# A MoE down projection turned round: tokens stationary, w_down streamed in two fp32r halves

## The reference

```
logits = xf @ w_router + b_router;  top 4 of 32 experts, softmax over the four logits
gu     = x_e @ w_gate_up[e] + b_gate_up[e]                 # 1024 -> 2048, gate and up interleaved
gate   = min(gu[:, 0::2], 7);  up = clip(gu[:, 1::2], -7, 7)
hidden = (up + 1) * gate * sigmoid(1.702 * gate)
y      = hidden @ w_down[e] + b_down[e]                    # 1024 -> 1024
out[token] += weight * y
```

## Time and profile before

| | us |
|---|---|
| median of 3 runs (2374.33 to 2377.72) | 2376.84 |
| the profiled execution | 2372.35 |
| its span in the trace | 2370.5 |
| TensorE busy (matmul) | 2273.3 (96%) |
| VectorE busy | 941.1 (40%) |
| ScalarE busy | 460.3 (19%) |
| GpSimd busy | 225.1 (9%) |
| down product, line 1064 | 514.7 in 4096 instructions |
| gate and up, line 1053 | 1037.6 in 8192 instructions |

### The profile page before, as it was taken

The page is one execution under the profiler, slowest core; times in us unless marked ns, Lnnn a source line. Parts: engine busy times, 40 slices in busy tenths (PEclk is TensorE's granted clock), DMA queues, the critical chain, the costliest instruction groups (busy, mean ns, idle before and its releaser), DMA issues.

```text
span 2370.5 us, 43566 instructions
## 1 busy us (share of the span) xinstructions
PE 2273.3 (96%) x17841; PEld 2164.4 (91%) x17842; DVE 941.1 (40%) x2192; ACT 460.3 (19%) x848; POOL 225.1 (9%) x172
## 2 busy tenths in 40 slices
PE   6999999999969999999999999999999999999997
PEld 5878888777869999999999999999999999999997
DVE  6434434875363333233333333433333332333332
ACT  4243143664101111111111111111111111111110
POOL 1101101100000100001010001100010110001001
PEclk9999999999979999999999999999999999999998
DMA  4222222105378887788888877886888886888882
GB/s 163 98 71 72 89 89 65 62 2 186 114 234 265 270 284 237 236 272 268 288 277 288 278 239 248 274 278 220 289 271 283 271 265 216 286 290 272 287 271 36
DMA packets 250615, 504.05 MB, mean 213 GB/s; under 512 B 7994, under 2 KB 36718, under 8 KB 250238
## 3 DMA queue, kind: packets, MB, share of 16 engines
q1 hardware_dynamic: 234268, 451.96, 54.9%
q0 software_dynamic: 14912, 45.71, 9.7%
q10 hardware_dynamic: 1344, 5.01, 0.7%
HBM read 469.46 MB, written 31.10 MB: 211 GB/s over the span
## 4 chain that ended last, share of the span: by engine, by line
PE 91%; DVE 4%; issue 3%; DMA 1%; ACT 0%; POOL 0%; DVEq 0%; ACTq 0%; SPq 0%; POOLq 0%
PE bank L1053 43%; PE bank L1064 19%; PE bank L804 12%; PE bank L1041 3%; DVE hx L1413 2%; PE bank L1012 2%; PE bank L921 2%; PE bank L908 2%; PE bank L956 1%; PE bank L958 1%; PE bank L957 1%; PE bank L1004 1%; PE bank L886 1%; PE bank L812 1%; PE bank L898 0%
## 5 line engine op out<-in xcount | busy, mean ns | idle before, releaser
L1053 PE MATMUL bank<-hx,ring 128*128 128x140 f32 (+1 forms) x8192 | 1037.6, 288 | 26.2 <-issue 16.7
L1053 PEld LDWEIGHTS bank<-hx,ring 128*128 128x128 f32 x8192 | 1021.4, 197 | 33.2 <-issue 32.2
L1064 PE MATMUL bank<-hx,ring 128*128 128x140 f32 (+1 forms) x4096 | 514.7, 287 | 0.0
L1064 PEld LDWEIGHTS bank<-hx,ring 128*128 128x128 f32 x4096 | 507.0, 190 | 0.0
L760 ACT ACTIVATE hx<-hx 128x168 f32<-128x168 f32 x256 | 87.9, 343 | 1447.0 <-DVE hx L1484 1447.0
L1484 DVE TENSOR_SCALAR hx<-bank,hx 128x168 f32<-128x168 f32 x256 | 100.4, 392 | 639.4 <-PE bank L1053 638.9
L1509 DVE TENSOR_SCALAR hx<-bank,hx 128x168 f32<-128x168 f32 x256 | 100.5, 392 | 353.8 <-PE bank L1064 353.8
L573 POOL DMA_INDIRECT out_x<-mix,hx x66 | 99.8, 1513 | 825.4 <-ACT mix L753 780.9
L552 POOL DMA_INDIRECT mix<-xn_scratch,hx x66 | 64.7, 981 | 718.8 <-DVE hx L1408 708.7
L804 PE MATMUL bank<-hx_r,mix_r 128*128 128x512 f32 x480 | 116.1, 401 | 7.9 <-DVE hx_r L1147 7.9
L804 PEld LDWEIGHTS bank<-hx_r,mix_r 128*128 128x128 f32 x480 | 92.1, 193 | 28.4 <-issue 9.2
(11 more groups left out here) (202 smaller groups left out, 1697.8 us busy)
## 6 DMA issues: line engine op xcount, KB each, us to landing
ring<-in_w_gate_up SPq DMA_DIRECT2D x128, 2048.0 KB, 10.8
ring<-in_w_down SPq DMA_DIRECT2D x64, 2048.0 KB, 8.8
mix<-in_w_in SPq DMA_DIRECT2D x14, 1024.0 KB, 5.0
work<-in_w_in SPq DMA_DIRECT2D x14, 1024.0 KB, 5.0
ring<-in_x SPq DMA_DIRECT2D x8, 512.0 KB, 8.2
hx<-in_w_out SPq DMA_DIRECT2D x1, 4096.0 KB, 14.1
work<-in_x ACTq DMA_DIRECT2D x8, 512.0 KB, 4.8
out_x<-work SPq DMA_DIRECT2D x8, 512.0 KB, 4.4
```

The costliest lines, as they stand in the source:

```text
L1053: mm = e.matmul(bank[f % 2][:, part * CAP:part * CAP + w], gu_ring[:, k, f * 256 + part:(f + 1) * 256:2], xT[:, k, 0:w], start=k == 0, sto ...
L1064: return e.matmul(bank[2 + j % 2][:, 0:w], dn_ring[:, k, j * P:(j + 1) * P], hid[:, k, 0:w], start=k == 0, stop=k == KD - 1)
```

## The change

The down product is turned round, and with it what comes before and behind.

- CAP grows from 168 to 192 = 128 + 2 x 32; the widths are 140, 168 and 192. All evictions of gate and up are 192 wide. The one-hot table has 3 x 128 columns in place of 168: one set for the first 128 tokens, and for each of two overflow groups of 32 tokens the same 32 four times.
- Down product, first 128 tokens: the tokens' hidden (128x128) is stationary, w_down streams 512 output columns at a time, split as upper + lower fp32r parts: 3 products for each of 8 k and 2 halves t (48 in place of 64 fp32 ones). The result is token by feature, so that `turn_rows` goes. The bias comes from one product with a selector row per half.
- ScalarE copies w_down's upper part (8 copies of 128x1024 in steps f = 3 to 6) and the hidden's (8 of 128x128); VectorE subtracts for the lower parts.
- Tokens past 128: for each overflow group, 32 tokens stationary in four column groups of the array, one per quarter of the output, plain fp32, 256 columns moving; under a branch on the token count.
- The gather is three indirect DMAs: 128 rows of 4 KB, and for each overflow group 128 quarter rows of 1 KB; so is the scatter-add. GpSimd now gathers for the next block ahead of the scatter of this one, whose rows lie in the same memory (y_m over xg).
- Both w_down slices are loaded once the whole down product of the block before is done.
- `turn_tokens` stands in the second half of the down product, ahead of its last four k.
- The tables of the loop move from `mix` to `hx` and `small`, and `mix` and `work` hold the two halves of w_down.

```diff
-CAP = 168
-HC = CAP // 2
+OV = 32
+GR = P // OV
+RO = 2
+CAP = P + RO * OV
+NH = 1 + RO
-WIDTHS = (140, CAP)
+WIDTHS = (140, 168, CAP)
...
                 for c in range(2):
-                    e.wait_ge(m_dn, n * 8 + (4 * c - 4))
+                    e.wait_ge(m_dn, n * 2 + 2)
                     e.dma_start(dn_ring[:, :, c * 512:(c + 1) * 512], dn_r[x_e, c]).then_inc(dn_in[c], 16)
...
             def gather():
+                e.indirect_dma_start(out=xg, out_offset=None, in_=xn_dram,
+                                     in_offset=bass.IndirectOffsetOnAxis(ap=idx[:, 0:1], axis=0)).then_inc(g_in, 16)
+                for r in range(RO):
+                    e.indirect_dma_start(out=xg_o[:, r], out_offset=None, in_=xn_quarters,
+                                         in_offset=bass.IndirectOffsetOnAxis(ap=idx[:, 1 + r:2 + r], axis=0)).then_inc(g_in, 16)
...
             def block_dmas(n):
-                add_rows(n)
                 e.wait_ge(l_ok, n + 2)
-                e.wait_ge(g_tr, n * 3 + 3)
+                e.wait_ge(sc_done, n * 48 + 48)
                 e.sem_inc(pool_go, 1)
                 gather()
+                add_rows(n)
...
+            def upper(n, q):
+                nh, k = q // 4, q % 4 * 2
+                if k == 0:
+                    e.wait_ge(dn_in[nh], n * 16 + 16)
+                e.activation(dn_hi[:, nh, k:k + 2], dn_ring[:, k:k + 2, nh * CH:(nh + 1) * CH], ACT.Copy).then_inc(c_hi, 1)
+
             def weigh_rows(n):
+                e.wait_ge(l_keep, n + 1)
+                e.wait_ge(g_tr, n * 4 + 8)
+                for t in range(2):
+                    e.wait_ge(m_dn, n * 2 + (t + 3))
+                    e.activation(y_m[:, t * CH:(t + 1) * CH], bank[2 + t][:, :], ACT.Copy, scale=w_sc[:, 0:1]).then_inc(m_yo, 1)
+                for r in range(RO):
+                    e.activation(y_o[:, r], bank[7][:, r * 2 * P:(r + 1) * 2 * P], ACT.Copy,
+                                 scale=w_sc[:, 1 + r:2 + r]).then_inc(m_yo, 1)
             def block_act(n):
                 for f in range(KD):
                     e.wait_ge(m_gate, n * 8 + (f + 1))
                     e.wait_ge(m_gs, n * 8 + (f + 1))
                     e.activation(sg[:, f % 2], g1[:, f % 2], ACT.Sigmoid, scale=GALPHA).then_inc(m_sig, 1)
-                    if f == 0:
-                        weigh_rows(n)
+                    if 3 <= f < 7:
+                        upper(n, 2 * f - 6)
+                        upper(n, 2 * f - 5)
+                    e.wait_ge(m_hid, n * 8 + (f + 3))
+                    e.activation(hid_hi[:, f], hid[:, f, 0:P], ACT.Copy).then_inc(h_hi, 1)
+                weigh_rows(n)
...
+            def over_bias():
+                for r in range(RO):
+                    for j in range(GR):
+                        e.matmul(bank[7][quarter_rows(j), r * 2 * P:(r + 1) * 2 * P], sel[:, 0:OV],
+                                 bias_d[:, j * 2 * P:(j + 1) * 2 * P], start=r == 0, stop=False, skip_group_check=True)
+            def down_main(n, t, k):
+                if t == 0:
+                    e.wait_ge(h_lo, n * 8 + (k + 1))
+                if k % 2 == 0:
+                    e.wait_ge(c_lo, n * 8 + (4 * t + k // 2 + 1))
+                for h, w in ((hid_hi, dn_hi), (hid_lo, dn_hi), (hid_hi, dn_lo)):
+                    mm = e.matmul(bank[2 + t][:, :], h[:, k], w[:, t, k], start=False, stop=k == KD - 1 and w is dn_lo,
+                                  skip_group_check=True)
+                if k == KD - 1:
+                    mm.then_inc(m_dn, 1)
+            def down_over(r):
+                for k in range(KD):
+                    for j in range(GR):
+                        e.matmul(bank[7][quarter_rows(j), r * 2 * P:(r + 1) * 2 * P],
+                                 hid[:, k, P + r * OV:P + (r + 1) * OV], dn_ring[:, k, j * 2 * P:(j + 1) * 2 * P],
+                                 start=False, stop=k == KD - 1, skip_group_check=True)
...
+                e.wait_ge(s_sel, n + 1)
+                down_bias(0)
+                for k in range(KD):
+                    down_main(n, 0, k)
+                down_bias(1)
+                for k in range(4):
+                    down_main(n, 1, k)
+                e.wait_ge(g_in, n * 48 + 96)
+                turn_tokens()
+                for k in range(4, KD - 1):
+                    down_main(n, 1, k)
+                e.wait_ge(l_ok, n + 2)
+                over_bias()
+                with e.If(tokens > P):
+                    down_over(0)
+                if w > P + OV:
+                    with e.If(tokens > P + OV):
+                        down_over(1)
+                down_main(n, 1, KD - 1)
...
+            def lower(n, q):
+                nh, k = q // 4, q % 4 * 2
+                e.wait_ge(c_hi, n * 8 + (q + 1))
+                e.tensor_tensor(dn_lo[:, nh, k:k + 2], dn_ring[:, k:k + 2, nh * CH:(nh + 1) * CH],
+                                dn_hi[:, nh, k:k + 2].bitcast(F32), ALU.subtract).then_inc(c_lo, 1)
+            def hidden_low(n, f):
+                e.wait_ge(h_hi, n * 8 + (f + 1))
+                e.tensor_tensor(hid_lo[:, f], hid[:, f, 0:P], hid_hi[:, f].bitcast(F32), ALU.subtract).then_inc(h_lo, 1)
...
+                    if f:
+                        hidden_low(n, f - 1)
                     e.wait_ge(m_sig, n * 8 + (f + 1))
...
+                    if 3 <= f < 7:
+                        lower(n, 2 * f - 6)
+                        lower(n, 2 * f - 5)
                     if f == 6:
...
+                hidden_low(n, KD - 1)
+                for m in range(4):
+                    e.wait_ge(g_tr, n * 4 + (m + 5 if m < 2 else 8))
+                    tokens_out(m)
```

More of the change, by code:

```diff
@@ L62 @@
 GALPHA = 1.702
-C_ID, C_MB, C_BO, C_LS, C_ON, C_CA = (P * i for i in range(6))
+C_ID, C_ON, C_MB, C_BO, C_LS, C_CA = (P * i for i in range(6))
 C_IO = 6 * P
-C_I32 = C_IO + CAP
+C_I32 = C_IO + NH * P
 C_TID = C_I32 + NE
@@ L88, in constants @@
     t[:, C_CA:C_CA + P] = r <= c
-    t[:, C_IO:C_IO + CAP] = np.arange(CAP)
+    t[:, C_IO:C_IO + NH * P] = np.concatenate([np.arange(P)] + [P + OV * j + np.arange(P) % OV for j in range(RO)])
+    t[:, C_SEL:C_SEL + NE + 1] = r % NE == np.arange(NE + 1)[None, :]
+    t[:, C_J] = np.arange(P) // OV
     t[:, C_I32:C_I32 + NE] = np.arange(NE)
@@ L427, in layer @@
+        idx_sc = small[:, 764:764 + NH].bitcast(U32)
+        w_sc = small[:, 768:768 + NH]
+        sel = small[:, 776:840].bitcast(BF16)[0:3 * NE]
+        bias_d = cst[:, C_MB:C_MB + D // 2].bitcast(BF16)[0:3 * NE]
+        hot = region(work[:, 8192:9728].bitcast(BF16), 0, NT, NH * P)
         f_a = region(work[:, 9216:9728].bitcast(BF16), 0, NT, 4, NE)
         f_b = region(work, 0, NT, 4, NE)
-        f_n = region(work, 8192, NT, NE)
-        f_r = region(work, 8448, NT, NE)
-        f_c = region(work, 8704, NT, NE)
+        f_t = region(work, 1024, NT, NE)
@@ L558, in _ @@
             e.wait_ge(e_st[1], 128)
-            e.dma_start(b_rows[:, 2048:3072], b_down[0]).then_inc(sc_done, 16)
+            for g in range(3):
+                e.dma_start(b_raw[g * NE:(g + 1) * NE], b_down[0]).then_inc(sc_done, 16)
             e.wait_ge(l_ok, 1)
@@ L1001, in token_list @@
             def token_list():
[L1002 removed]
+                for h in range(NH):
                     for i in range(NT):
[L1004 removed]
+                        mm = e.matmul(bank[7][:, 5 * h:5 * h + 5], hot[:, i, h * P:(h + 1) * P], tw_s[:, i, :],
                                       start=i == 0, stop=i == NT - 1)
@@ L1444, in _ @@
             e.wait_ge(bias_ok, 3)
-            for m in range(3):
-                e.wait_ge(g_tr, m + 1)
+            for g in range(1, 3):
+                e.wait_ge(b_cast, g)
+                rows = slice(0, 3 * NE) if g == 1 else slice(2 * NE, 3 * NE)
+                e.tensor_tensor(b_raw[rows], b_raw[rows], bias_d[rows], ALU.subtract).then_inc(b_sub, 1)
+            for m in range(4):
+                e.wait_ge(g_tr, m + 1 if m < 2 else 4)
                 tokens_out(m)
-            for s_ in (m_up, m_gs, m_hid):
+            for s_ in (m_up, m_gs, m_hid, m_dn):
                 e.sem_inc(s_, 2)
+            e.sem_inc(m_yo, 4)
             grid = [P, NX, NE]
```

254 lines of the change are left out of this document (113 added, 141 removed).

## The result

The changed kernel takes 2360.17 us (median of 5 runs, 2358.24 to 2364.68), the kernel before 2376.84 in the same series (5 runs, 2370.44 to 2377.72). The ratio is 0.9943, its 95% interval 0.9927 to 0.9958. The span of the profiled execution fell from 2370.5 to 2358.3 us, the mean granted clock from 0.981 to 0.972. The forecast was 37 us slower.

The account below looks back on a forecast made before the run. TensorE (96% busy) was taken as the bound, its savings then spent waiting for gathered tokens. Blocks +0.6, clock +34 and +4, surroundings -2 gave +37 us on 2372.35: 2409, or 2414 as a median; range 2310 to 2500.

Parts of the forecast that it names:

- TensorE's work: Expert loop: by TensorE alone a block to 128 tokens takes 44.8 us, 48.4 with overflow, the overflow 3.6.
- two at a time: Rival, overflow products: column groups overlap only in pairs, 6.9 us each, 63 us more, 2477; chance 0.10.
- one at a time: Rival, overflow products: column groups don't overlap, 13.8 us each, 194 us more, 2608; chance 0.06.
- VectorE and ScalarE: Gate-up stage: table and splitting make steps 3 to 6 4.25 us each, so indices stand at S + 35.35.
- The gather: Ahead of the token turning: tokens land 9.0 us after the indices, at S + 44.35; TensorE waits 2.75 us.
- the gather lands early: Rival, ahead of the turning: tokens 7.6 us after indices, wait 1.3 us, 2328, or no wait, 2292; chance 0.20.
- The clock: Behind the 2.75 us wait: clock falls in three of four narrow blocks, 1.7 us each, 34 us; wide ones 4.
- The sum: Whole kernel: regular blocks 1656.3 us against 1655.7, plus clock and surroundings, +37 us in all.
- the start: Ahead of the loop: shorter bias turning, b_down casts and a later ScalarE start cost 0, at worst +5 us.
- the tail: After the loop: the last back-transposition goes (3.8 us counted), a third scatter comes (1.51 + 0.30): -2 us.
- w_down late: Rival, down-weight loads issued after the whole down product: 2 us lost in each block, 2478; chance 0.05.
- nothing felt: Rival, expert loop: no VectorE or GpSimd work delays TensorE, loop 1533 us, time 2252; chance 0.04.

Follow-up runs that it names:

- list5: Changed kernel with the next block's token list read out in step f = 5, ahead of that step's w_down subtractions, instead of f = 6: 2310.94 us, 0.974.
- two_bodies: Changed kernel with the loop body of width 192 left out, so widths 140 and 168 only: 2327.77 us, 0.9792.
- late_w: Changed kernel with both w_down slices issued only after slice f = 0 of the same block's gate-up is done: 2416.31 us, 1.0179.
- list5_two: Changed kernel with the token list read out in step f = 5 and only the widths 140 and 168: 2284.32 us, 0.9632.
- early_list: Changed kernel with the token list read out in step f = 6 ahead of the two w_down subtractions instead of behind them: 2345.28 us, 0.9867.
- late_list: Changed kernel with the token list read out in step f = 7, behind that step's evictions, instead of f = 6: 2394.58 us, 1.0078.
- unsplit: Changed kernel with the down product as 16 plain fp32 products instead of 48 fp32r ones, without the splitting copies and subtractions: 2391.77 us, 1.0085.

## Why the prediction was wrong

By its own steps.

**TensorE's work: right.** Rates and counts held: list5, where TensorE doesn't wait for tokens, runs at 45.14 and 48.58 us where 44.8 and 48.4 were worked out. The overflow took 3.46 us where 3.6 was taken and 3.45 was the lower end; four column groups run wholly beside each other. The chances given to two at a time and one at a time (0.16 together) had the value product's row against them, rightly. The estimate by the Trainium skill (TensorE: Matmul & The Clock Gate, Packing small matmuls), 4.4 us from its 2.38x for three column tiles, was too high: 13.8/3.46 is 4.0x here.

**VectorE and ScalarE: right.** Steps 3 to 6 were 4.07 us apart (4.25), step 2 took 5.9 with the table (6.0), the indices stood at S + 34.6 (35.35, so 0.75 sooner). The splitting took 1.22 us as in the earlier trace rows, the table 3.35. TensorE waited once for the low hidden, 0.45 us, where 1.45 was counted.

**The gather: the first step that failed.** "I take the 9.0 that was seen." The wait was 1.0 to 1.6 us in place of 2.75. The text had what was needed: it saw that the weights' stream ends at about S + 40 and so covers "only the start of the gather", and then took the value of a gather at the start of the loop all the same. The runs show 9.3 to 9.6 us where the stream covers the whole and 7.5 where it ends 2.0 us before the landing. So the tokens stood at S + 42.1 in place of 44.35: 1.5 us by this step, 0.75 by the earlier indices. As the block ends 4.6 us behind the tokens, it took 46.65 in place of 49.05 and 50.3 in place of 52.65, and the regular blocks 1589 in place of 1656.3: 67 us. The rival "the gather lands early" had such a gather (7.6 us from the indices) and such a wait (1.3 us) at a chance of 0.20; its block of 47.65 us is still 1.0 too long, most of it the 0.75 of the indices.

**The clock: failed with it.** 34 + 4 us were counted for falls behind that wait, and in plain blocks none came. The term itself is real: at 2.15 us of wait the clock fell in 8 of 20 blocks, at 3.17 in 14 of 20, and a fall cost 1.6 us (1.7 had been read from the earlier trace rows). What was wrong was above all its input, the length of the wait; the three in four counted for 2.75 us are also more than either of these two shows.

**What the prediction did not have: the third body.** The change of WIDTHS from two to three was quoted and given no price. The pauses for "issue" behind the wide blocks were in the earlier trace rows as 2.2 us and were used for the clock alone; what they are was not asked. More than that, the sum dropped them: each of the five 60.87 us of before holds a pause of 2.20, 11.0 in all, while the 56.3 and 59.9 set against them hold none. They grew from 12.8 to 52.4 us. two_bodies shows the cause by taking 32.4 us away. Its 2328 is also the number of the rival "the gather lands early", but by luck: there blocks that are 1.0 us too long stand for pauses that the rival doesn't have.

**The sum.** In the spans, +36.6 us was predicted and -12.2 came, 48.8 less: 67.2 by the regular blocks and 38 by the clock. Against them stand 52.4 of pauses; 16.0 for block 0 and the slow clock behind pauses, set against the 15.1 by which the loop of before (1670.8) was itself longer than the 1655.7 taken; and 3.1 by the start, 3.0 later (inside "0, and at worst +5"), and the tail (-1.9 for -2). The first three of these are larger than the effect itself, and their sum, not their sizes, gave the sign. The range of 2310 to 2500 held the time; the sign did not hold. The other rivals: w_down late did not come (its halves landed at S + 8.8 and 18.5, and late_w shows 1.9 us a block and the clock for 4 us of delay), nothing felt, 2252, is approached by list5_two: 2284, of which 22.0 are pauses.

## What to carry to other kernels

A transfer's time is not a number of its own: read where it stands against the bulk stream beside it, and take the latency of the case that matches (here 9.3 to 9.6, 7.5 or 6.3 us from the indices for the same three gathers). When work is added ahead of the instruction that starts a long chain (indices, gather, turning), put that instruction first: moving six small VectorE instructions a step ahead, and in front of that step's splitting, gave 49 us, three times what the whole change gave. And count the bodies of a loop as a cost: pauses for "issue" behind the wide blocks are there in the trace of before, and one more body can make them four times as long.

## What the runs showed of the hardware

- Four column groups of 32, fp32 with 256 columns moving, run fully beside each other (64 instructions in 3.46 us, 4.0 times the rate of one after another), but only when neighbours in the order go to different groups; with the same instructions grouped by column group it is 11.3 us.
- Three indirect gathers, issued within 2.7 us, landed 9.3 to 9.6 us after their indices beside a stream of weights at some 385 GB/s, and 6.3 us after them where the third was issued 0.4 us before the stream ended (list5, early_list and late_w against late_list). The third alone took 5.7 us from its issue in list5 and 2.8 in late_list.
- Behind a wide block TensorE stopped for 2.5 to 3.0 us when its program had two bodies in the loop (once not at all), and behind the narrow one that follows for 3.4 to 4.5. With three bodies it was 10.3 to 17.4 behind wide blocks (behind the second of two in a row 2.8 to 3.1, but 10.4 in unsplit), 7.6 in place of 10.6 to 10.9 when 4 MB of loads were not issued at that moment, and 5.2 to 5.7 when the stage ahead of it was 7.8 us longer. In the three pauses read packet by packet TensorE started 3.1 to 3.5 us behind the last packet of the code queue.
- The clock fell behind waits of 2.0 to 2.4 us in some blocks and not in others of equal work; what decides between them the runs don't show.
